# One encoder layer on one core: weights, mixing coefficients and a bias table stored as long runs per partition

## The reference

```
mod = silu(c) @ ada_w + ada_b                  # c: 1024, ada_w: 1024 x 6144; six vectors per group
h   = rms_norm(x) * (1 + scale1) + shift1
z   = h @ w_in                                 # w_in: 1024 x 3456
a   = neighbourhood_attention(q, k, v, bias)   # first 1536 columns of z, 8 heads of 64
r   = rwkv7(token_shift(z_r, mu), ...)         # other 1920 columns, mu: 2 x 1920, both directions
x   = x + gate1 * (concat(a, r) @ w_out)
h   = rms_norm(x) * (1 + scale2) + shift2
x   = x + gate2 * moe(h)                       # best of 4 groups, 2 of its 8 experts, hidden width 512
y   = rms_norm(x)
```

## Time and profile before

| | |
|---|---|
| time, median of 3 runs | 1389.93 us (1388.32 to 1390.71) |
| profiled execution, span from first to last instruction | 1375.9 us |
| its own time beyond the span | not listed by the page; the median is 14.0 us above the span |
| TensorE busy | 1178.5 us (86%) |
| VectorE, ScalarE, GpSimd busy | 421.8, 348.6, 280.7 us |
| moved by DMA | 314.74 MB in 82025 packets, mean 229 GB/s |
| expert weights | 96 loads of 2048 KB |
| modulation weights | 12 loads of 2048 KB |
| projection weights | 11 slabs of 1024 KB, one of 512 KB, values 2048 KB |

### The profile page before, as it was taken

One profiled execution on the slowest core, in us unless ns is written; L12 is line 12 of the kernel. 1 busy time (PEld: TensorE's weight loads), 2 busy tenths in 40 slices (PEclk: granted clock), 3 DMA queues, 4 the chain that ended last, 5 costly groups with the idle time before them and its releaser, 6 DMA issues.

```text
span 1375.9 us, 29721 instructions
## 1 busy us (share of the span) xinstructions
PE 1178.5 (86%) x13063; PEld 727.2 (53%) x13063; DVE 421.8 (31%) x742; ACT 348.6 (25%) x749; POOL 280.7 (20%) x254
## 2 busy tenths in 40 slices
PE   5899999999997898988899958997788878888765
PEld 3555555555454787877755535554444444444432
DVE  2100043434565555666437361000000000000017
ACT  3200024353323554565532111110010010010003
POOL 0100012221326343367412001111111111111000
PEclk9999999999997899999999978999999999999987
DMA  9894231122435211221407169999999999999966
GB/s 319 325 337 164 69 94 62 54 82 72 153 123 141 68 39 38 50 57 27 172 7 310 70 262 327 398 390 397 401 404 405 408 404 404 398 395 396 411 270 249
DMA packets 82025, 314.74 MB, mean 229 GB/s; under 512 B 13808, under 2 KB 28488, under 8 KB 65150
## 3 DMA queue, kind: packets, MB, share of 16 engines
q1 hardware_dynamic: 75862, 298.96, 58.5%
q0 software_dynamic: 5120, 12.59, 2.6%
q10 hardware_dynamic: 936, 1.61, 0.3%
HBM read 291.58 MB, written 25.74 MB: 231 GB/s over the span
## 4 chain that ended last, share of the span: by engine, by line
PE 28%; DMA 27%; DVE 5%; ACT 4%; issue 3%; SPq 1%; POOL 0%; DVEq 0%; POOLq 0%; ACTq 0%
DMA arena<-in_exp_w 26%; PE bank L1585 10%; PE bank L2472 6%; PE bank L1855 6%; PE bank L2490 2%; PE bank L1609 2%; SPq L2326 1%; DVE arena L1466 1%; PE bank L2211 1%; PE bank L2459 1%; DMA arena<-pick_out 1%; DVE arena L1453 1%; DVE arena L2577 0%; ACT arena L1295 0%; DVE arena L1483 0%
## 5 line engine op out<-in xcount | busy, mean ns | idle before, releaser
L2472 PE MATMUL bank<-arena 128*64 128x256 f32 x2048 | 256.8, 409 | 67.9 <-DMA arena<-in_exp_w 58.1
L907 PE MATMUL bank<-arena 128*128 128x512 f32 (+1 forms) x736 | 256.3, 497 | 4.4 <-POOL arena L493 1.6
L2472 PEld LDWEIGHTS bank<-arena 128*64 128x64 f32 x2048 | 158.7, 147 | 175.4 <-DMA arena<-in_exp_w 70.0
L1585 PE MATMUL bank<-arena 64*64 64x64 f16 (+3 forms) x7184 | 204.7, 221 | 36.4 <-issue 12.6
L1585 PEld LDWEIGHTS bank<-arena 64*64 64x64 f32 (+2 forms) x7184 | 183.2, 127 | 63.6 <-issue 35.9
L907 PEld LDWEIGHTS bank<-arena 128*128 128x128 f32 x736 | 133.9, 189 | 99.4 <-issue 85.0
L2490 PE MATMUL bank<-arena 128*64 128x512 f32 x512 | 118.6, 605 | 17.5 <-ACT arena L2416 17.5
L2438 DVE TENSOR_TENSOR arena<-bank,arena 128x256 f32<-128x256 f32 x32 | 13.6, 424 | 303.5 <-PE bank L2472 303.5
L2363 POOL DMA_INDIRECT arena<-h_scratch,arena x32 | 30.8, 962 | 362.5 <-PE bank L2459 260.7
L1855 PE MATMUL bank<-arena 128*128 128x512 f32 x192 | 86.4, 597 | 0.0
L2490 PEld LDWEIGHTS bank<-arena 128*64 128x64 f32 x512 | 34.8, 137 | 79.3 <-issue 55.7
(11 more groups left out here) (262 smaller groups left out, 1285.9 us busy)
## 6 DMA issues: line engine op xcount, KB each, us to landing
arena<-in_exp_w SPq DMA_DIRECT2D x96, 2048.0 KB, 44.7
arena<-in_ada_w SPq DMA_DIRECT2D x12, 2048.0 KB
arena<-in_w_in SPq DMA_DIRECT2D x11, 1024.0 KB, 6.6
direction_scratch<-arena SPq DMA_DIRECT2D x6, 1536.0 KB, 5.9
arena<-direction_scratch SPq DMA_DIRECT2D x24, 384.0 KB, 5.4
arena<-pick_out SPq DMA_DIRECT2D x6, 1024.0 KB, 10.1
arena<-in_x_sample SPq DMA_DIRECT2D x8, 512.0 KB, 5.0
arena<-in_w_out SPq DMA_DIRECT2D x8, 512.0 KB, 6.4
```

The costliest lines, as they stand in the source:

```text
L907: return nc.tensor.matmul(bank[i % 3][:, 0:GR[p] * GW], w[:, k, :], hT[:, k, PART[p]], start=(k == 0), stop=(k == KD - 1))
L1585: return nc.tensor.matmul(out, lhsT, r, start=start, stop=True, skip_group_check=True)
L2472: ins = nc.tensor.matmul(bank[b + 2 * c.s][BLK * n:BLK * n + BLK, 0:HALF], xT[c.s][:, j, :], slot[c.w][:, j, n * HALF:(n + 1) * HALF], sta ...
```

## The change

All of it is layout. The host stores `ada_w` chunk by chunk, in each chunk partition by partition, so that one partition's part of a chunk is one run of 4096 floats. `w_in` is stored tile by tile (128 columns) and then partition by partition: one run of 1024 floats for each tile and partition; the slab on chip has the tile as its outer index, so that TensorE still reads 128 neighbouring floats per row. The value weights get an array of their own, `w_v`, one run of 4096 floats per partition. The coefficients are stored with a third column of zeros, which VectorE overwrites as before. The prompt's bias gets an array of its own and comes by one DMA. The values on chip, the order of the queue and the products are as before; the wait for the bias counts two DMAs and not seven.

```diff
-        slab = [take(KD * 2 * P).rearrange("p (k n) -> p k n", k=KD) for _ in range(NSLAB)]
+        slab = [take(KD * 2 * P).rearrange("p (h k n) -> p h k n", h=2, k=KD) for _ in range(NSLAB)]
...
-        ada_v = A["ada_w"][0].rearrange("(k p) n -> p k n", p=P)
-        win_v = A["w_in"][0].rearrange("(k p) n -> p k n", p=P)
...
-                sp.dma_start(adaw[i % NADA], ada_v[:, :, c * 512:(c + 1) * 512]).then_inc(sem(f"wide_in{i % NADA}"), 16)
+                sp.dma_start(adaw[i % NADA], A["ada_w"][c]).then_inc(sem(f"wide_in{i % NADA}"), 16)
...
-                sp.dma_start(slab[i % NSLAB][:, :, 0:n * P], win_v[:, :, col:col + n * P]).then_inc(sem(f"slab_in{i % NSLAB}"), 16)
+                sp.dma_start(slab[i % NSLAB][:, 0:n], A["w_in"][col // P:col // P + n].rearrange("h p k n -> p h k n")).then_inc(sem(f"slab_in{i % NSLAB}"), 16)
...
-            sp.dma_start(mu[:, :, 0:2], A["mu"]).then_inc(sem("cols_in"), 16)
+            sp.dma_start(mu, A["mu"]).then_inc(sem("cols_in"), 16)
...
-            sp.dma_start(wv, win_v[:, :, 2 * W:3 * W]).then_inc(sem("wv_in"), 16)
+            sp.dma_start(wv, A["w_v"]).then_inc(sem("wv_in"), 16)
...
-            for k in range(3):
-                src = A["bias"][k][0:64].rearrange("p (h e) c -> e p h c", e=2)
-                for e in range(2):
-                    sp.dma_start(bias_p[64 * e:64 * e + 64, k], src[e][:, :, 0:4 * KB]).then_inc(sem("bias_p_in"), 16)
+            sp.dma_start(bias_p, A["bias_p"]).then_inc(sem("bias_p_in"), 16)
...
-                    dve.wait_ge(sem("bias_p_in"), 16 * 7)
+                    dve.wait_ge(sem("bias_p_in"), 16 * 2)
...
-                return slab[s % NSLAB][:, :, hf * P:(hf + 1) * P]
+                return slab[s % NSLAB][:, hf]
...
-    a["mu"] = np.ascontiguousarray(a.pop("rwkv_mu")[0].reshape(2, NZ, P).transpose(2, 1, 0))
+    mu = a.pop("rwkv_mu")[0].reshape(2, NZ, P).transpose(2, 1, 0)
+    a["mu"] = np.ascontiguousarray(np.concatenate([mu, np.zeros_like(mu[:, :, :1])], 2))
+    a["ada_w"] = np.ascontiguousarray(a["ada_w"][0].reshape(KD, P, 12, W).transpose(2, 1, 0, 3))
+    w_in = a.pop("w_in")[0].reshape(KD, P, -1, P)
+    a["w_in"] = np.ascontiguousarray(w_in.transpose(2, 1, 0, 3))
+    a["w_v"] = np.ascontiguousarray(w_in[:, :, 8:12].reshape(KD, P, W).transpose(1, 0, 2))
...
+    pairs = a["bias"][:, 0:64, :, 0:4 * KB].reshape(3, 64, NPAIR, 2, 4 * KB)
+    a["bias_p"] = np.ascontiguousarray(pairs.transpose(3, 1, 0, 2, 4).reshape(P, 3, NPAIR, 4 * KB))
```

## The result

The changed kernel takes 1378.84 us (median of 10 runs) against 1384.86 for the kernel before (10 runs beside it): 0.9945 [0.9923, 0.9967], which is the ratio of the two times with its 95% interval. Measured again in experiment e1 the ratio is 0.9960 [0.9942, 0.9977]. So it is faster, by 5.5 to 7.6 us after the two ratios and by 6.0 and 3.5 us after the two pairs of medians (e1: 1383.76 and 1380.31). Now and then an execution of either kernel takes 1941 to 6307 us (one of these 10, and four of those in and beside the experiments), and such times count in the medians but not in the ratios. The forecast was 1385.6, and the time lies under its range, which began at 1383.4.

A forecast was written before the change was run, and what follows sets the result against it. Bound taken: TensorE's DMA waits in the first 60 us, then expert weights at an unchanged rate. Gains 2.03 (coefficients) + 0.15 (modulation) + 0.4 (slab) + 1.7 (clock) = 4.3 us; 1389.93 - 4.3 = 1385.6 us, range 1383.4 to 1390.4.

The forecast's parts named there:

- The base: Starting time of the whole kernel: 1389.93 us, the median of the runs, from which the 4.3 us gain was subtracted.
- The coefficients: Load ahead of the second modulation chunk: 1,920 runs of 8 B become 128 of 180 B, gaining 2.03 us.
- the hole: DMA rate falls to 119 GB/s from 14 to 16.5 us, during the coefficients' load; claimed to go.
- SP's stall: SP's issue of the second modulation chunk took 7.53 us; claimed to fall under 1 us.
- rival C: Small coefficients' load keeps its price, or SP stalls anyway; only 0.15 + 0.4 gained, 1389.4 us; chance 0.16.
- The modulation chunks: Two chunks ahead of TensorE's wait, 4.2 MB, at 400 GB/s instead of 394: 0.15 us gained.
- The projection slab: First projection waited for its weights until 27.22 us, though TensorE could start at about 26.8: 0.4 us gained.
- The clock: Granted clock at 0.51 from 28 to 31.5 us, on the first projection; taken as gone, 1.7 us gained.
- the dip: The stretch of low granted clock, 28 to 31.5 us, costing 1.7 us; claimed gone as TensorE idles less.
- rival B: The low clock on the first projection stays, since TensorE still idles twice: 1387.3 us; chance 0.27.
- The sum and the barrier: Terms add to 4.3 us; whatever is gained before 60 us should reach the barrier whole.
- Rival D: Expert weights may lie elsewhere in memory and stream slower; at 2% slower, 1394.5 us; chance 0.12.

The follow-up runs named there:

- e2: Kernel before with only the mixing coefficients repacked into long runs (128 of 180 B): 1381.12 us, ratio 0.9976.
- e5: Kernel before, old layouts, with only the mixing coefficients' load moved behind the sixth modulation chunk: 1380.69 us, ratio 0.9971.
- e4: Kernel before with only value weights and prompt bias as own arrays, in the changed kernel's memory order: 1385.23 us, ratio 1.0010.
- e8: Kernel before, unchanged, measured again against itself: 1384.12 us, ratio 0.9995.
- e13: Kernel before with 48 tiny products added at TensorE's start, no gap filled: 1377.25 us, ratio 0.9931.
- e12: Changed kernel with 21 products filling only TensorE's three later gaps (at 40, 53 and 56 us): 1378.83 us, ratio 0.9953 to the kernel before.
- e14: Changed kernel with 48 tiny products added at TensorE's start, no gap filled: 1370.72 us, ratio 0.9884 to the kernel before.
- e3: Changed kernel with the mixing coefficients loaded as before (1,920 runs of 8 B): 1382.72 us, ratio 0.9991 to the kernel before.
- e15: Changed kernel with its TensorE gaps filled (32 products) and 16 tiny products at the start: 1368.95 us, ratio 0.9878 to the kernel before.

## Why the prediction was wrong

**The base, the step that failed.** The prediction subtracted from 1389.93 us, "the median of the runs, 1389.93, is 14.0 more, and nothing of that is touched". That median of three was taken as the kernel's level with a spread of 1.2, and the 14.0 us above the span as a constant part of the time. Beside the experiments the kernel before was run about 110 times: its medians were 1383.8, 1384.6, 1384.9, 1385.2 and 1385.8, and its single runs lay between 1377 and 1395. So the three runs stood 5 us above its level, and their narrow spread didn't show it. The miss of 6.8 us is 5.1 of base (1389.93 - 1384.86) and 1.7 of gain (the two medians differ by 6.0, the forecast by 4.3). That the gain was forecast too small is not shown as clearly as the base: by the medians e1 has 3.5 us, and its interval (3.2 to 8.0 us) holds 4.3. The 14.0 us were in sight; that span and time of one execution lie only about 2 us apart came out with the later runs. It suggests that the profiled run and the three timed ones came from opposite ends of a wide spread, which can't be shown, since the former's own time isn't on record. With 1384.9 as base the forecast would have been 1380.6, beside the 1378.84 and 1380.31 of the two measurements.

**The coefficients: right.** e2 and e5 both take away the hole and SP's stall, one by long runs and one by place. Their second chunk starts at 21.13 and 21.01, against 22.86 to 24.19 where the short runs stand ahead (before, e4, e8, e13): 1.7 to 3.2 us for a term of 2.03. That refutes rival C. The Trainium skill ("DMA: Bandwidth & Descriptors", Anatomy of one DMA and Rules for kernel authors) gives a DMA a fixed cost and says that one under 64 KB pays mostly overhead. That its form therefore wouldn't matter was the prediction's reading, and it is not borne out here: 0.9976 for the form alone (e2).

**The modulation chunks: mis-sized.** I took 400 GB/s from the expert stream, a gain of 0.15 us. (Two of each three expert loads have the one run of 16 KB that I read there; the third has two of 8 KB per partition, L1885.) In the profile after, the stretches of the front ran at 419 to 425. The 4.2 MB that took 10.64 us at 394 would take 10.0 at 420, so I estimate the term at 0.65; most marks fit it (21.0 to 21.1 in e2 and e5, 20.2 to 20.4 in after, e1 and e12). One does not: in e14, which has the same loads, the second chunk starts at 21.54, behind a wait of 2.35 us, though its stretches ran at 436, 392 and 420 GB/s. Why it came late there is open.

**The projection slab: a race, not a term.** Its wait is gone after, but also in e2, where the slab has its old runs, and in e4, e8 and e13, which all wait 1.01 us for VectorE there. In e5 it is late by 0.65 us (1.66 against 1.01). In the profile of before it is late by 0.27 (1.28 against 1.01) and not by the 0.4 us read there, and in other executions of the same front not at all.

**The clock: the sign right, the account wrong.** "I take the dip as gone" holds up to 41 us in both profiles of the changed kernel (after, e1), but in one of them falls come at 41.2 and 58.3, in the other none. And it fails in e12 and e14, the changed kernel with products added only later or only at the start: the clock is low for 3.4 us from 25.6 and from 21.9 us, on the first projection and on the second chunk:

```profile
24.24 8.80 PE L902 MATMUL bank<-arena 128*128 128x512 f32 x16 [1.01 <-DVE arena L488]
```

```profile
21.54 3.38 PE L867 MATMUL bank<-arena 128*32 128x128 f32 x64 [2.35 <-DMA arena<-in_ada_b]
```

With the coefficients ahead and the gaps unfilled the low clock around these two lasts 3.4, 3.4, 6.8, 10.2 and 13.7 us (e3, before, e4, e13, e8), beside waits of 2.77, 3.23, 3.70, 4.64 and 4.80 us for the second chunk. The wait alone doesn't settle it: e12 has its fall behind 0.67 us, e5 none there behind 1.59. While TensorE is at work, half of such a stretch is lost. So the dip that I priced at 1.7 was among the mildest, and rival B, the dip that stays, holds in some executions and not in others. B's argument that the idle times shrink to a third was also true of the first alone (3.23 to 0.65; 1.28 to 1.01 in the profile after).

**The sum and the barrier.** The value products end, near 140 us, at 143.2 in the mean of the profiles with a front like before's (before, e4, e8, e13) and at 138.4 in those like after's (after, e1, e14): 4.7 us. Their last group in before and in after:

```profile
133.65 7.15 PE L942 MATMUL bank<-arena 128*128 128x512 f32 x16
```

```profile
131.71 7.15 PE L937 MATMUL bank<-arena 128*128 128x512 f32 x16
```

The first products behind the barrier start at 435.2 and 430.8 in the same means: 4.4 us. The runs give 5.5 to 7.6 us, and e1's interval holds both. That a gain before 60 us reaches the end is so borne out in the mean of several profiles, and not in each pair. The parts agree too: 3.3 for the coefficients (e2) and 1.2 for all else (e3, an interval that holds nought). Rival D is refuted: from 900 to 1300 us the expert stream runs at 401 GB/s before and after, and e4 is no slower.

**Open.** Why 48 products more, at any of the places tried ahead of it, make the second program some 7 us shorter. The clock doesn't tell the two kinds apart: over that stretch it is 0.93 to 0.95 in the eight profiles and 0.93 to 0.94 in the five. TensorE's recurrence products (7184 of them; busy, mean ns, idle ahead of them and what ended most of it) in the page of the kernel before, of the changed one and of e15:

```profile
L1585 PE MATMUL bank<-arena 64*64 64x64 f16 (+3 forms) x7184 | 204.7, 221 | 36.4 <-issue 12.6
```

```profile
L1580 PE MATMUL bank<-arena 64*64 64x64 f16 (+3 forms) x7184 | 201.9, 219 | 40.5 <-issue 15.2
```

```profile
L1591 PE MATMUL bank<-arena 64*64 64x64 f16 (+3 forms) x7184 | 200.8, 219 | 34.3 <-issue 11.0
```

The idle time ahead of these products is 36.4 to 42.0 us in the eight profiles without added products, 36.1 to 38.8 in the four with 21 to 32, and 33.4 to 35.3 in the five with 48. Between the eight and the five that is 39.8 against 34.4 us in the mean, so most of the 7 us is there. The part of it in which TensorE waited for nothing that the profile shows ("issue") is 12.6 to 17.6, 13.0 to 15.7 and 10.2 to 11.9 us. The long gaps, counted in the traces, also move with the number of added instructions: between the weight loads of the recurrence behind 448 us there are 6 to 10 gaps over 1 us without added products, 4 to 5 with 21 to 32, and 3 to 4 with 48, and in each of the 17 profiles one stands near the 9012th or the 9138th weight load since TensorE's start, whatever number of products was added. A gap is so tied to a count of instructions and not to a product, which fits e13's expectation that it matters where TensorE's blocks of instructions begin. What is waited for in these gaps no run here shows.

## What to carry to other kernels

Look for the few kilobytes that are written as thousands of tiny runs ahead of a load that an engine waits for: they are read from a hole in the DMA rate with the engines busy, and from a long issue in the queue behind them, and moving them is worth as much as repacking them. Before a number is subtracted from a time, compare the profiled execution's span with the timed runs: where they lie far apart, the kernel's spread may be as wide as that, and a few more runs of the kernel before are worth more than another term of the sum. And when added instructions make a kernel faster, run the same number of them where they can do nothing, before the place gets the credit.

## What was not expected of the hardware

Forty-eight tiny products at TensorE's start shorten a program that begins 430 us later from 397.3 us (mean of eight profiles) to 390.0 (of five with 48 products, these tiny ones alone in two of them), and the kernel before by 8.5 us (0.9931; 1385.77 against 1377.25). The stretch at the low clock varies fourfold between two executions of one kernel (3.4 us in before, 13.7 in e8). The front, whose loads are mostly chunks in runs of 16 KB, ran at 419 to 425 GB/s in the profile after, but the expert stream, in runs of 16 and 8 KB, at 401.
